# A decoder layer on one core: opening reordered, segment sums moved from TensorE to GpSimd

## The reference

```
h   = rms_norm(x) * g_mix
q, k, v, z, xbc, dt, gates = split(h @ w_in)
# 8 attention heads, each with two softmaxes p1, p2 over (q.k + bias), causal
o   = (p1 - lam * p2) @ v,  normalised per head
# 32 state-space heads in 8 groups of 4, in 4 chunks of 128 tokens
a     = softplus(dt + dt_bias) * (-exp(a_log))
acum  = cumsum(a) within the chunk
decay = exp(acum[l] - acum[s]) where s <= l, else 0
y     = (C B^T * decay * dt) @ x + (C @ state) * exp(acum) + d_skip * x
state = state * exp(a_end) + B^T @ (x * exp(a_end - acum) * dt)
```

## Time and profile before

| | |
|---|---|
| median of 3 runs | 2227.08 us (2225.8 to 2227.1) |
| the profiled execution | 2225.09 us |
| its span, first to last instruction | 2223.3 us |
| mean granted clock of TensorE | 0.962 |
| PE, PEld, DVE, ACT, POOL busy | 2064.5, 1671.8, 1587.5, 1364.7, 576.3 us |
| opening up to the first projection | 0 to 51.2 us |
| first three projections | 51.2 to 71.1 us |
| eight mixer steps | 71.1 to 697.4 us |
| output projections, norm, routing, experts | 702.4 us to the end |

### The profile page before, as it was taken

The page is one execution under the profiler, slowest core; times in us unless marked ns, Lnnn a source line. Parts: engine busy times, 40 slices in busy tenths (PEclk is TensorE's granted clock), DMA queues, the critical chain, the costliest instruction groups (busy, mean ns, idle before and its releaser), DMA issues.

```text
span 2223.3 us, 30784 instructions
## 1 busy us (share of the span) xinstructions
PE 2064.5 (93%) x9582; PEld 1671.8 (75%) x9582; DVE 1587.5 (71%) x1644; ACT 1364.7 (61%) x1612; POOL 576.3 (26%) x444
## 2 busy tenths in 40 slices
PE   4999999998997999882999999999999999999996
PEld 4877777776775888771788888888888888888885
DVE  3466557557556333324799999999999999999995
ACT  4465656656556222321677777777777777777774
POOL 0111111201210000003053434434353434434351
PEclk7999999999997999985999999999999999999998
DMA  4121222122011222442899999999999999999994
GB/s 141 48 88 38 68 68 69 37 68 87 30 39 48 95 99 99 145 170 94 313 355 386 366 390 365 385 374 385 377 377 382 369 390 363 389 374 375 383 377 158
DMA packets 111145, 509.28 MB, mean 229 GB/s; under 512 B 17888, under 2 KB 20488, under 8 KB 78344
## 3 DMA queue, kind: packets, MB, share of 16 engines
q1 hardware_dynamic: 102280, 479.03, 56.8%
q0 software_dynamic: 8832, 29.84, 6.0%
HBM read 489.01 MB, written 20.91 MB: 229 GB/s over the span
## 4 chain that ended last, share of the span: by engine, by line
PE 51%; DVE 1%; issue 0%; ACT 0%; DMA 0%; POOL 0%; POOLq 0%; ACTq 0%; DVEq 0%
PE bank L1621 32%; PE bank L1634 16%; PE bank L1599 1%; PE bank L1610 1%; PE bank L1645 1%; PE bank L1656 1%; DVE w_lo L1751 0%; DMA keep<-h_rows,g_idx 0%; ACT w_hi L1692 0%; DVE keep L1766 0%; DVE x_lo L1681 0%; DVE keep L1763 0%; DVE keep L1770 0%; POOL out_rows L1840 0%; DVE a_lo L1681 0%
## 5 line engine op out<-in xcount | busy, mean ns | idle before, releaser
L1751 DVE TENSOR_TENSOR w_lo<-big,w_hi 128x2048 fp32r<-128x2048 f32 x384 | 875.8, 2288 | 86.1 <-ACT w_hi L1692 80.3
L1692 ACT ACTIVATE w_hi<-big 128x2048 fp32r<-128x2048 f32 x384 | 736.8, 1920 | 228.5 <-PE bank L1621 174.4
L1621 PE MATMUL bank<-w_hi,x_hi 128*128 128x512 f32 x1024 | 279.7, 395 | 2.6 <-DVE w_lo L1751 2.6
L1621 PE MATMUL bank<-w_lo,x_hi 128*128 128x512 f32 x1024 | 275.5, 391 | 0.0
L1621 PE MATMUL bank<-w_hi,x_lo 128*128 128x512 f32 x1024 | 275.0, 390 | 0.0
L1621 PEld LDWEIGHTS bank<-w_hi,x_hi 128*128 128x128 f32 x1024 | 191.0, 189 | 53.3 <-DVE w_lo L1751 14.7
L1621 PEld LDWEIGHTS bank<-w_lo,x_hi 128*128 128x128 f32 x1024 | 193.4, 189 | 40.7
L1621 PEld LDWEIGHTS bank<-w_hi,x_lo 128*128 128x128 f32 x1024 | 193.2, 189 | 40.3
L1829 POOL CAST pick<-pick_rows 128x112 fp32r x65 | 18.3, 282 | 598.1 <-PE bank L1634 573.3
L986 PE MATMUL bank<-h_hi,wm_hi 128*128 128x512 f32 x384 | 162.9, 424 | 5.8 <-DVE h_lo L772 5.8
L1634 PE MATMUL bank<-w_hi,a_hi 128*128 128x512 f32 x512 | 162.2, 398 | 0.0
(11 more groups left out here) (261 smaller groups left out, 3573.4 us busy)
## 6 DMA issues: line engine op xcount, KB each, us to landing
big<-in_w SPq DMA_DIRECT2D x384, 1024.0 KB, 8.6
big<-in_w_mix SPq DMA_DIRECT2D x72, 512.0 KB, 3.3
keep<-in_w_tail SPq DMA_DIRECT2D x47, 512.0 KB, 3.3
keep<-in_x SPq DMA_DIRECT2D x4, 512.0 KB, 7.4
big<-in_x SPq DMA_DIRECT2D x4, 512.0 KB, 5.1
out_rows<-keep SPq DMA_DIRECT2D x4, 512.0 KB, 3.8
h_rows<-keep SPq DMA_DIRECT2D x4, 512.0 KB, 3.7
bias_rows<-dist_rows SPq DMA_DIRECT2D x1, 1024.0 KB
```

The costliest lines, as they stand in the source:

```text
L1621: ins = pe.matmul(bank[c][:], x_part, w_part[:, s, c * 512:(c + 1) * 512], start=False, stop=n == W1_PAIRS - 1 and w_part is w_hi and x_pa ...
L1692: act.activation(w_hi[:, place(b, at_n, SPLIT)], raw[:, place(b, at_n, RAW)], ACT.Copy).then_inc(hi_ready.sem, 1)
L1751: dve.tensor_tensor(w_lo[:, s], raw[:, place(b, at_n, RAW)], w_hi[:, s].bitcast(F32), ALU.subtract).then_inc(lo_ready.sem, 1)
```

## The change

- SP's loads are put in another order: x tiles 0 and 1, the identity alone, the small tables, x tiles 2 and 3, weight piece 0, and the rest behind; separate semaphores stand for identity, small tables, bias rows and the other constants.
- ACT only forms 1/rms (mean_square); the DVE scales x (scale_x). h_hi and h_lo are made per token tile between the others' steps (high, low). Six PSUM banks take the turned tiles instead of two. The dt projection stands behind project(0,0), its softplus behind taps(0,0).
- The segment sums: a fourth product at L996 gives the cumulative sums turned (head by token), these go to DRAM (acum_rows), and one DMA for each chunk and step reads four rows of it to all 128 partitions into seg[u]. POOL subtracts the sum of its own token and multiplies with the triangle, both in place; ACT takes the exponential in place and the DVE multiplies the masked C B^T on in place. The 32 products of `seg` are gone from PE. Each chunk has a buffer; two of them lie where decay and mix were, one where am was, one in an unused part of dT.
- SP issues the segment loads of the next step between the weight pieces (SEG_AT), behind ydiag_ready of the chunk. In the opening its list has: wait for acum_ready, write, wait, four loads, then piece 8.
- masked_cb writes its product twice side by side, so that make_mix runs over 2 x 256 instead of 4 x 128.
- make_diff(2) stands ahead of sum_y(2), make_diff(3) ahead of taps(i+1,0).

The diff without declarations, renamed waits (apart) and the new names of buffers; indentation is cut by twelve:

```diff
+SEG_AT = {4: (0, 1), 6: (2,), 8: (3,)}
...
+acum_rows = nc.dram_tensor("acum_rows", (NT, HEADS, HPG * P), F32, kind="Internal").ap()
...
-    sp.dma_start(cst[:], consts).then_inc(consts_in, 16)
-    sp.dma_start(smalls[:], small).then_inc(consts_in, 16)
-    for t in range(NT):
+    def x_tile(t):
         sp.dma_start(xin[:, t * D:(t + 1) * D], x_rows[t * P:(t + 1) * P, :]).then_inc(x_in[t], 16)
+    x_tile(0)
+    x_tile(1)
+    sp.dma_start(cst[:, 0:P], consts[:, 0:P]).then_inc(ident_in, 16)
+    sp.dma_start(smalls[:], small).then_inc(small_in, 16)
+    x_tile(2)
+    x_tile(3)
+    sp.dma_start(mraw[:, 0], w_mix[0, 0]).then_inc(piece_in[0].sem, 16)
+    sp.dma_start(conv.rearrange("p a b -> p (a b)")[0:32, 0:HEADS], rel_bias).then_inc(dist_in, 16)
+    sp.dma_start(conv[0:32, 2, 0:GL], onehot_rows).then_inc(dist_in, 16)
     sp.dma_start(dT.rearrange("p a b -> p (a b)")[:, 0:KT * SSM_H], w_dt).then_inc(wdt_in, 16)
+    sp.dma_start(mraw[:, 1], w_mix[0, 1]).then_inc(piece_in[1].sem, 16)
+    sp.dma_start(cst[:, P:2 * P], consts[:, P:2 * P]).then_inc(consts_in, 16)
+    sp.dma_start(cst[:, 2 * P:4 * P], consts[:, 2 * P:4 * P]).then_inc(consts_in, 16)
+    sp.dma_start(cst[:, 4 * P:N_CONST], consts[:, 4 * P:N_CONST]).then_inc(consts_in, 16)
     sp.dma_start(par_sb[:], par).then_inc(consts_in, 16)
-    sp.dma_start(conv.rearrange("p a b -> p (a b)")[0:32, 0:HEADS], rel_bias).then_inc(consts_in, 16)
-    sp.dma_start(conv[0:32, 2, 0:GL], onehot_rows).then_inc(consts_in, 16)
-    for p in range(MRAW):
-        sp.dma_start(mraw[:, p], w_mix[0, p]).then_inc(piece_in[p].sem, 16)
+    sp.dma_start(mraw[:, 2], w_mix[0, 2]).then_inc(piece_in[2].sem, 16)
+    def load_seg(i, u):
+        rows = acum_rows[u, bass.ds(i, 1)] if not isinstance(i, int) else acum_rows[u, i:i + 1]
+        src = rows.to_broadcast([P, HPG * P])
+        if u == 3:
+            src = src.rearrange("p (a n) -> p a n", a=2)
+        sp.dma_start(flat_seg(u), src).then_inc(seg_in[u].sem, 16)
+    def load(p):
+        sp.wait_ge(plo_ready.sem, plo_ready.at(0, p - MRAW + 1))
+        sp.dma_start(mraw[:, p % MRAW], w_mix[0, p]).then_inc(piece_in[p % MRAW].sem, 16)
     sp.wait_ge(dist_read, 1)
     sp.dma_start(dist_rows, conv[0:HEADS, 1, 0:GL]).then_inc(dist_out, 16)
+    load(3)
     sp.wait_ge(dist_out, 16)
     sp.dma_start(bias_rows, toeplitz(dist_rows)).then_inc(dist_out, 16)
+    for p in range(4, 8):
+        load(p)
     sp.wait_ge(dist_out, 32)
     sp.dma_start(biasT[:], bias_rows[0]).then_inc(bias_in.sem, 16)
-    for p in range(MRAW, PIECES):
-        sp.wait_ge(plo_ready.sem, plo_ready.at(0, p - MRAW + 1))
-        sp.dma_start(mraw[:, p % MRAW], w_mix[0, p]).then_inc(piece_in[p % MRAW].sem, 16)
+    sp.wait_ge(acum_ready, 1)
+    sp.dma_start(acum_rows.rearrange("c s (h l) -> (c s h) l", h=HPG), cbm[:, 0:P]).then_inc(acum_out, 16)
+    sp.wait_ge(acum_out, 16)
+    for u in range(NT):
+        load_seg(0, u)
+    load(8)
     with sp.Fori(0, HEADS - 1) as i:
         for p in range(PIECES):
+            for u in SEG_AT.get(p, ()):
+                sp.wait_ge(ydiag_ready.sem, ydiag_ready.at(i, u + 1))
+                load_seg(i + 1, u)
             sp.wait_ge(plo_ready.sem, plo_ready.at(i + 1, p - MRAW + 1))
             sp.dma_start(mraw[:, p % MRAW], w_mix[bass.ds(i + 1, 1), p].rearrange(
                 "a p n -> (a p) n")).then_inc(piece_in[p % MRAW].sem, 16)
...
...
-            pool.tensor_tensor(am, bcast_mid(tri, HPG), bcast_inner(heads(a_all, u), P),
-                               ALU.mult).then_inc(am_ready.sem, 1)
+            pool.wait_ge(seg_in[u].sem, seg_in[u].at(i, 1))
+            acum = heads(a_all, u)
+            if u < 3:
+                acum = bcast_inner(acum, P)
+            else:
+                acum = acum.rearrange("p (a b) -> p a b", a=2).unsqueeze(3).to_broadcast([P, 2, 2, P])
+            pool.tensor_tensor(seg[u], seg[u], acum, ALU.subtract).then_inc(seg_sub.sem, 1)
+            pool.wait_ge(seg_sub.sem, seg_sub.at(i, u + 1))
+            causal = (bcast_mid(tri, HPG) if u < 3
+                      else tri.unsqueeze(1).unsqueeze(1).to_broadcast([P, 2, 2, P]))
+            pool.tensor_tensor(seg[u], seg[u], causal, ALU.mult).then_inc(am_ready.sem, 1)
...
         act.wait_ge(x_in[t], 16)
-        ch.link(act.activation(sqx, xt, ACT.Square, accum_out=st[:, t:t + 1]))
+        ch.link(act.activation(sqx, xin[:, t * D:(t + 1) * D], ACT.Square, accum_out=st[:, t:t + 1]))
+        if t == 0:
+            act.wait_ge(eps_ready, 1)
         ch.link(act.activation(st[:, t:t + 1], st[:, t:t + 1], ACT.Ln, bias=eps[:, 0:1], scale=1.0 / D))
-        ch.link(act.activation(st[:, t:t + 1], st[:, t:t + 1], ACT.Exp, scale=-0.5))
-        act.activation(xt, xt, ACT.Copy, scale=st[:, t:t + 1]).then_inc(h_ready, 1)
-    act.wait_ge(lam_ready, 2)
-    ch.link(act.activation(lam_t[:, HD:HD + 2], lam_t[:, HD:HD + 2], ACT.Exp))
-    act.activation(ez[:, 0:SSM_H], sm("a_log"), ACT.Exp).then_inc(lam_ready, 1)
-    for b in range(2 * NT):
-        t, half = b // 2, b % 2
-        act.wait_ge(hT_read, b + 1)
-        r = (slice(None), slice(4 * half, 4 * half + 4), slice(t * P, (t + 1) * P))
-        act.activation(h_hi[r], hT[r], ACT.Copy).then_inc(hhi_ready, 1)
+        act.activation(st[:, t:t + 1], st[:, t:t + 1], ACT.Exp, scale=-0.5).then_inc(rms_ready, 1)
+    def high(t):
+        for half in range(2):
+            act.wait_ge(hT_read, 2 * t + half + 1)
+            r = (slice(None), slice(4 * half, 4 * half + 4), slice(t * P, (t + 1) * P))
...
-    for p in range(3):
-        split(0, p)
+    mean_square(0)
+    mean_square(1)
+    mean_square(2)
+    high(0)
+    mean_square(3)
+    high(1)
+    high(2)
+    split(0, 0)
+    high(3)
+    split(0, 1)
+    split(0, 2)
+    act.wait_ge(lam_ready, 1)
+    ch.link(act.activation(lam_t[:, HD:HD + 2], lam_t[:, HD:HD + 2], ACT.Exp))
+    act.activation(ez[:, 0:SSM_H], sm("a_log"), ACT.Exp).then_inc(lam_ready, 1)
+    act.wait_ge(hT_banks, 2 * NT)
+    split(0, 3)
+    act.wait_ge(dist_read, 1)
+    act.wait_ge(consts_in, 64)
+    tap(0, 0)
     act.wait_ge(dt_read, 1)
     ch.link(act.activation(eacum[:], wend[:], ACT.Exp, scale=-1.0))
     act.activation(eacum[:], eacum[:], ACT.Ln, bias=1.0).then_inc(dt_read, 1)
-    act.wait_ge(hT_banks, 2 * NT)
-    for p in range(3, 6):
-        split(0, p)
-    act.wait_ge(dist_out, 32)
-    tap(0, 0)
+    split(0, 4)
+    split(0, 5)
+    act.wait_ge(dist_out, 16)
     tap(0, 1)
     split(0, 6)
     split(0, 7)
...
-            act.wait_ge(seg_ready.sem, seg_ready.at(i, u + 1))
-            act.wait_ge(mix_ready.sem, mix_ready.at(i, u))
-            act.activation(decay.rearrange("p a b -> p (a b)"), seg_b[:], ACT.Exp).then_inc(
-                decay_ready.sem, 1)
+            act.wait_ge(am_ready.sem, am_ready.at(i, u + 1))
+            act.activation(flat_seg(u), flat_seg(u), ACT.Exp).then_inc(decay_ready.sem, 1)
...
+        dve.wait_ge(rms_ready, t + 1)
+        xt = xin[:, t * D:(t + 1) * D]
+        dve.tensor_scalar(xt, xt, st[:, t:t + 1], None, ALU.mult).then_inc(h_ready, 1)
+    def take_hT(t):
+        for half in range(2):
+            b = 2 * t + half
+            dve.wait_ge(hT_banks, b + 1)
+            if b == 0:
+                dve.wait_ge(small_in, 16)
+            dve.tensor_tensor(hT[:, 4 * half:4 * half + 4, t * P:(t + 1) * P],
+                              hT_bank(b)[:].rearrange("p (a b) -> p a b", a=4),
+                              bcast_inner(smalls[:, 4 * half:4 * half + 4], P), ALU.mult).then_inc(hT_read, 1)
+    def low(t):
+        r = (slice(None), slice(None), slice(t * P, (t + 1) * P))
+        dve.wait_ge(hhi_ready, 2 * (t + 1))
+        dve.tensor_tensor(h_lo[r], hT[r], h_hi[r].bitcast(F32), ALU.subtract).then_inc(hlo_ready, 1)
...
+    scale_x(0)
+    scale_x(1)
+    take_hT(0)
+    scale_x(2)
+    take_hT(1)
+    low(0)
+    scale_x(3)
+    take_hT(2)
+    low(1)
+    take_hT(3)
+    low(2)
+    split(0, 0)
+    low(3)
+    dve.wait_ge(dist_ready, 1)
+    ch.link(dve.tensor_copy(conv[0:HEADS, 1, 0:GL], s_b[0][0:HEADS, 0:GL]))
+    ch.link(dve.tensor_copy(far[:], s_b[1][:, 0:HEADS]))
+    dve.memset(conv[0:HEADS, 1, 256:GL], NEG).then_inc(dist_read, 1)
+    ch.link(dve.tensor_tensor_reduce(lam_t[:, 0:HD], sm("lq1"), sm("lk1"), 1.0, 0.0, ALU.mult, ALU.add,
+                                     lam_t[:, HD:HD + 1]))
+    dve.tensor_tensor_reduce(lam_t[:, 0:HD], sm("lq2"), sm("lk2"), 1.0, 0.0, ALU.mult, ALU.add,
+                             lam_t[:, HD + 1:HD + 2]).then_inc(lam_ready, 1)
+    split(0, 1)
+    split(0, 2)
+    ch.link(dve.tensor_scalar(sm("qg"), sm("qg"), HD ** -0.5, None, ALU.mult))
+    ch.link(dve.tensor_scalar(sm("subg"), sm("subg"), 1.0 - LAMBDA_INIT, None, ALU.mult))
+    dve.wait_ge(lam_ready, 2)
+    ch.link(dve.tensor_tensor(eps[:, 2:3], lam_t[:, HD + 1:HD + 2], lam_t[:, HD:HD + 1], ALU.subtract))
+    ch.link(dve.tensor_scalar(eps[:, 2:3], eps[:, 2:3], -LAMBDA_INIT, None, ALU.add))
```

(55 more changed lines are left out.)

93 lines of the change are left out of this document (33 added, 60 removed).

## The result

The changed kernel takes 2207.98 us (median of 4 runs, 2207.06 to 2210.46), beside 2227.09 for the kernel before on the same chip (4 runs, 2225.80 to 2227.47). The ratio is 0.9917, with an interval of 0.9900 to 0.9934: 19.1 us faster. The forecast was 47.7 us faster, 2179.4, with a range of 2159 to 2200. The sign was right, the size was not: 40% of the forecast gain came, and the time lies 8 us outside the range.

A forecast was written before the change was run, and what follows sets the result against it. The opening was taken as a chain of small steps, the loop as PE-bound apart from two waits a step. Terms 21.6 - 4.2 - 1.3 + 25 + 6.6 = 47.7; 2225.1 - 47.7 + 2.0 = 2179.4 us, range 2159 to 2200.

The forecast's parts named there:

- x first, h per tile: Opening: project(0,0) starts at 22, dt projection takes 7.5 us, project(0,3) at 49.5 instead of 71.1; gain 21.6.
- The path through DRAM: First step: load(8) behind the broadcasts lands at 57; PE waits 4.2 us before cb(0), plus 1.3 for low clock.
- rival B: Opening: loads late, dt at the low level, or load(8) at 61; 8 us less gain, 2187; chance 0.12.
- A step, segment products: Loop: seg(0) and seg(1) leaving PE gain 1.7 us a step; seg(2) and seg(3) bring nothing.
- A step, moves: Loop: earlier make_diff removes the 2.69 wait at the third turn_diff; project(i+1,2) starts 2.6 us earlier a step.
- POOL's port: Loop: doubled POOL work on segments holds up the DVE, costing 0.5 us a step.
- Rival D: POOL/DVE port: lengthened POOL operations hold up a DVE that is the bound, 96 us added, 2275; chance 0.03.
- Rivals C and E: C: all seg products and L1076 waits go, 2155, chance 0.10. E: seg stays on PE's path through POOL, 2206, 0.04.
- The last step: Last mixer step: make_diff(2) first gains 4.2, seg products 0.9 and 1.7, less 0.2 for the mask; 6.6 us.
- 25 us from the loop: Seven steps at 3.6 us each (1.7 + 2.6 - 0.26 - 0.5), a step of 75.5 us; bounds 1.0 and 6.5 a step.
- A step of 77 says A: Sign in the loop: a measured step of 77 us, not 75.5, would point to DVE and ACT setting the step.
- rival A: Loop: DVE and ACT set the whole step, so only seg(0) and seg(1) are gained; 2193; chance 0.16.

The follow-up runs named there:

- seg_own_rows: Changed kernel, each segment load reading 128 different DRAM rows instead of one for all partitions, decay left out of the computation: 2205.86 us, one run.
- fill: Changed kernel plus four unread products a step on PE, ahead of turn_y(0), turn_diff(3) and project(i+1,2): 2188.56 us, ratio 0.9833.
- seg_on_pe_fill: Changed kernel with segment sums back on PE and three unread products a step, ahead of turn_diff(3) and project(i+1,2): 2188.66 us, one run.
- undo_moves: Changed kernel with make_diff(2) back behind sum_y(2) and make_diff(3) behind taps(i+1,0): 2213.34 us, ratio 0.9946.
- before_fill: Kernel before the change plus four unread products a step, three ahead of turn_diff(2) and one ahead of turn_diff(3): 2224.54 us, ratio 0.9986.
- fill_project: Changed kernel with load(8) issued ahead of the acum_ready wait and two unread products a step, only ahead of project(i+1,2): 2175.85 us, one run.
- load8_fill: Changed kernel with load(8) issued ahead of the acum_ready wait and four unread products a step in front of PE's waits: 2178.31 us, ratio 0.9775.

## Why the prediction was wrong in size

By its own steps:

- **x first, h per tile.** Right: project(0,0) at 20.99 (22 forecast). The dt projection was mis-sized, 10.4 instead of 7.5: I named the low level as a bound and took the high one for the sum. The windows show 0.67 for it, though PE had no gap; with its 64 small products it was busy for 10.50 us out of 10.50. The same low stretch also made project(0,1) 1.8 us longer, which had no term. project(0,3) came at 52.4 instead of 49.5: 2.7 from start to start for dt and 1.8 for project(0,1), less 1.0 by which project(0,0) started early and 0.6 by which it was shorter than 8.2. One figure behind the forecast start was worked out wrongly: 2.6 MB in 7.4 us are 350 GB/s and not 260. Little hung on it, since project(0,0) came 1.0 early.
- **The path through DRAM.** Right as a chain, from SP over ACT's split to cb(0), and mis-sized: "lands at 57" was 65.6. Of the 8.6 us, 3.0 came with the issue (the late start of project(0,3) again, 2.9) and the rest from the transfer: 10.3 us from issue to landing, where I had put 4.7. I had taken the four broadcasts as 1 MB like any other; seg_own_rows shows that one row read by all partitions costs 4 us more. The low clock after the wait was put at 1.3 us; the waits of 9.1 and a cost of 12.5 leave 3.4. This step took 12.5 for 5.5, 7.0 of the 10.4 missing in the first stretch. With the 2.9 above that makes 9.9. What rival B names, a slow dt and a late load(8), came true, and was dearer than its 8 us.
- **A step, segment products.** 1.1 a step (fill against seg_on_pe_fill), where 1.7 less 0.26 and 0.5 made 0.94; but only 0.3 in the old order of the differences.
- **A step, moves.** Right in mechanism at a held clock: 2.8 for 2.6 behind the segment part, 2.0 ahead of it. The third turn_diff waits no more, and project(i+1,2) waits 1.8 for the taps. The forecast added the two parts as if they were independent; together they bring 3.1 for 3.5 at a held clock.
- **POOL's port.** About 0.7 for 0.5. Rival D is out: POOL's busy time rose by 52 us (576.3 to 628.3), more than the 33 forecast, mainly because the added product takes 1.3 to 1.5 us on average and not 1.04, and the time still fell. The Trainium skill (SBUF — State Buffer, SBUF: two separate sides) has a DVE operation in a two-port mode, or one with two SBUF inputs, blocked for the whole of a POOL instruction that came first. The row at 258.72, which ends with POOL's product, agrees; in which mode it ran, the trace doesn't say. It happens to one row a step, by 0.7 us.
- **Rivals C and E.** C wanted 7.1 a step, which no variant shows. E's price, 2206, lies near the measured 2208 by chance: the products are gone from PE, and no wait of PE for a segment stands in the loop's list above.
- **The last step.** The sum is right, 4.8 for 4.9, by luck. The moves brought 3.0 for 4.2 (undo_moves against after; the longest wait went from 5.7 to 2.7, not to 1.5), and the rest 1.8 for 0.7 (before against undo_moves). Both kernels run it at a low clock, 0.78 and 0.76, which the forecast didn't look at; with fillers it takes 38.5.
- **The step that failed: 25 us from the loop.** At 1.00 throughout, 75.5 a step came out as 75.65; this is closer than the terms deserve, since 0.35 of the 3.4 is low clock that before still has in its 79.07, and the parts make 3.1. What I left out is that I had replaced one wait of 2.69, followed by work that DVE and ACT bound anyway, by one of 1.8 directly ahead of the projections, which PE bounds. The prediction says that the wait is "handed over to project(i+1,2)" and charges nothing for it. In before the clock fell at the former place and cost 0.35 a step; in after it falls at the latter, for about 7 us in the later steps, and costs 2.0 a step on average (14.2 of the 15.2 us missing in the seven) and 2.8 where it is longest. I had looked at the granted clock in the opening and nowhere in the loop, where the earlier trace rows has 0.96 as a mean.

"A step of 77 says A" was a poor sign: two of the steps did take 77.2 and 77.3, and rival A is wrong. A sign has to be read together with the clock of the same window. The range allowed for one term at its bound and not for two: the steps alone at their lower bound (7 us in all; measured 9.8) give 2197, but the path through DRAM went beyond its own bound as well (waits of 9.1, for at most 8).

Open: why the second step of after has no low stretch though its waits are the same; what exactly lets the clock fall, since waits of 1.3 and 1.8 did in one place what 2.7 did in the other; and the 3.9 us of the tail. In the ten variants that compute the whole layer the tail, unchanged code, takes 1521.4 to 1526.5 us with no relation to the edit that I could find (before_fill has the longest, before with 1520.9 the shortest of these kernels). So I take the 3.9 for chance; that wasn't tested.

## What to carry to other kernels

Price a wait on TensorE by what comes behind it: here, ahead of work that TensorE bounds, 1.8 us of waiting cost up to 2.8 more in low clock; ahead of work that another engine bounds, 2.7 cost 0.35. Where an order moves the last wait of a step in front of its largest stretch of products, a few products that nobody reads, issued ahead of the wait, can be worth many times their effort (14 us in seven steps in fill, 17 in fill_project). Parts of a change whose gains end at the same wait are to be priced together: here they gave 3.1 a step together, and 0.3 or 1.1, and 2.0 or 2.8, depending on the order. And when a wait is put into a queue of transfers, look at what is issued behind it: one line, moving load(8) ahead, was worth 10 us.

## What the runs showed of the hardware that was not expected

- A low stretch without an idle engine: the 64 passes of 128x32 in the dt projection ran at a granted clock of 0.67 with PE busy for 10.50 of 10.50 us; it was 1.00 up to 32 us and 0.50 from 32.5 to 42 us, with PE busy all the while.
- A broadcast of one 2 KB row to 128 partitions (256 KB) is 3.7 to 4.5 us from issue to landing in the loop; four of them ahead of a 512 KB piece made it 10.3 us instead of 3.3, and 6.3 with 128 different rows.
- A filler of one 128x512 fp32 product costs nothing when it lies in a wait: steps of 75.61 to 75.69 with them, 75.69 for the one step of after that kept its clock without them.
- With the clock held, steps repeat within 0.1 us (fill, seg_on_pe_fill, fill_project; in load8_fill two of seven stand out by 0.5, behind a late weight piece); without, the same step takes 75.7 to 78.5.
